# Attention of a two-layer encoder: values with v as the stationary side, divided probabilities, outputs split at once, and a second attention whose head and first output products are interleaved

## The reference

```python
for layer in range(2):
    sh_m, sc_m, g_m, sh_f, sc_f, g_f = split(silu(c) @ ada_w[layer] + ada_b[layer], 6)
    h = rms_norm(x, norm_mix_g[layer]) * (1 + sc_m) + sh_m
    qa, ka, va, qd, kd, vd = split(h @ w_in[layer])          # 2304 columns; rotary on q and k
    ya = window_attention(...)     # 8 query heads of 64, 2 kv heads, +-128 tokens, a sink logit a head
                                   # p = exp(s - m) / (sum(exp(s - m)) + exp(sink - m));  p @ v
    yd = diff_attention(...)       # 4 heads: (softmax_1 - lam * softmax_2) @ v, v of 128 columns,
                                   # then rms_norm over 128 columns, * subln_g * (1 - lambda_init)
    x = x + g_m * (concat(ya, yd) @ w_out[layer])
    h = rms_norm(x, norm_ffn_g[layer]) * (1 + sc_f) + sh_f
    y = swiglu(h)                  # layer 0: dense, 3584 wide
    y = top-2-of-8 expert swiglu   # layer 1: expert weights of 3 x 1024 x 3584 each
    x = x + g_f * y
return rms_norm(x, final_g)
```

## Time and profile before

| what | value |
|---|---|
| time, median of 3 runs | 1364.37 us (1362.79 to 1368.64) |
| the profiled execution, time | 1363.22 us |
| its span in the trace | 1361.5 us |
| TensorE busy | 1288.9 us (95%) |
| VectorE busy | 452.0 us (33%) |
| ScalarE busy | 292.9 us (22%) |
| mean granted clock of TensorE | 0.984 of full speed |
| chain that ended last | PE 82%, DMA 9%, DVE 4%, SPq 2%, ACT 2% |
| traffic | 481.95 MB, mean 354 GB/s |

### The profile page before, as it was taken

One profiled execution on the slowest core, in us unless ns is written; L12 is line 12 of the kernel. 1 busy time (PEld: TensorE's weight loads), 2 busy tenths in 40 slices (PEclk: granted clock), 3 DMA queues, 4 the chain that ended last, 5 costly groups with the idle time before them and its releaser, 6 DMA issues.

```text
span 1361.5 us, 21859 instructions
## 1 busy us (share of the span) xinstructions
PE 1288.9 (95%) x9514; PEld 714.5 (52%) x9515; DVE 452.0 (33%) x808; ACT 292.9 (22%) x524; POOL 32.8 (2%) x82
## 2 busy tenths in 40 slices
PE   5999999999999989996689999999999999899997
PEld 5766888787888677441233333444354333244342
DVE  4876867777459665200100120001001110000011
ACT  3346544443433462110010000010010000010010
POOL 1102100000001010000000000000000000000000
PEclk9999999999999999998789999999999999899999
DMA  9988748888436757999999999999999999999996
GB/s 349 326 338 329 233 176 311 311 297 309 174 123 208 307 204 306 378 408 424 418 421 423 422 421 419 403 408 421 423 419 421 421 424 421 419 420 421 422 423 259
DMA packets 93044, 481.95 MB, mean 354 GB/s; under 512 B 8808, under 2 KB 10928, under 8 KB 63248
## 3 DMA queue, kind: packets, MB, share of 16 engines
q1 hardware_dynamic: 88992, 475.06, 86.9%
q10 hardware_dynamic: 2720, 2.93, 0.8%
q0 software_dynamic: 1232, 2.50, 0.8%
HBM read 477.32 MB, written 1.05 MB: 351 GB/s over the span
## 4 chain that ended last, share of the span: by engine, by line
PE 82%; DMA 9%; DVE 4%; SPq 2%; ACT 2%; issue 1%; POOL 0%; DVEq 0%; ACTq 0%
PE ps L2621 31%; PE ps L2671 15%; PE ps L2304 8%; PE ps L2306 8%; PE ps L2305 8%; DMA raws<-in_moe_w_down_dram 5%; DMA raw<-in_moe_w_gate_dram 2%; DMA weights<-in_ada_w_dram 2%; SPq L891 2%; PE ps L2687 2%; PE ps L2638 1%; DVE weights_lo L1376 1%; PE ps L2594 1%; PE ps L2385 1%; PE ps L2226 1%; PE ps L2370 1%
## 5 line engine op out<-in xcount | busy, mean ns | idle before, releaser
L2621 PE MATMUL ps<-raw,hX 128*32 128x384 f32 (+3 forms) x3840 | 473.0, 543 | 11.8 <-DMA raw<-in_moe_w_up_dram 8.4
L2621 PEld LDWEIGHTS ps<-raw,hX 128*32 128x32 f32 (+1 forms) x3840 | 162.0, 117 | 296.6 <-issue 267.3
L2671 PE MATMUL ps<-raws,m_actT 128*32 128x512 f32 (+1 forms) x1072 | 168.5, 604 | 9.9 <-DMA raws<-in_moe_w_down_dram 9.9
L2304 PE MATMUL ps<-weights_hi,hT_hi 128*128 128x512 f32 (+1 forms) x416 | 162.1, 390 | 2.6 <-DVE hT_lo L1482 1.4
L1797 DVE TENSOR_TENSOR m_act<-m_act,ps 128x512 f32<-128x512 f32 (+1 forms) x28 | 17.4, 621 | 432.0 <-PE ps L2621 431.2
L2306 PE MATMUL ps<-weights_hi,hT_lo 128*128 128x512 f32 (+1 forms) x416 | 159.0, 382 | 0.0
L2305 PE MATMUL ps<-weights_lo,hT_hi 128*128 128x512 f32 (+1 forms) x416 | 158.6, 381 | 0.0
L1376 DVE TENSOR_TENSOR weights_lo<-weights,weights_hi 128x2048 fp32r<-128x2048 f32 (+1 forms) x52 | 113.1, 2202 | 2.3 <-ACT weights_hi L1052 1.1
L2671 PEld LDWEIGHTS ps<-raws,m_actT 128*32 128x32 f32 (+1 forms) x1072 | 52.2, 123 | 116.3 <-issue 103.5
L1052 ACT ACTIVATE weights_hi<-weights 128x2048 fp32r<-128x2048 f32 (+1 forms) x48 | 87.2, 1840 | 55.9 <-PE ps L2306 51.3
L2304 PEld LDWEIGHTS ps<-weights_hi,hT_hi 128*128 128x128 f32 x416 | 78.2, 188 | 21.0 <-issue 4.8
(11 more groups left out here) (282 smaller groups left out, 1084.3 us busy)
## 6 DMA issues: line engine op xcount, KB each, us to landing
raw<-in_moe_w_gate_dram SPq DMA_DIRECT2D x64, 1024.0 KB, 16.5
raw<-in_moe_w_up_dram SPq DMA_DIRECT2D x64, 1024.0 KB, 22.1
raws<-in_moe_w_down_dram SPq DMA_DIRECT2D x32, 2048.0 KB, 24.7
raw<-in_moe_w_gate_dram SPq DMA_DIRECT2D x64, 768.0 KB, 23.3
raw<-in_moe_w_up_dram SPq DMA_DIRECT2D x64, 768.0 KB, 21.1
raws<-in_moe_w_down_dram SPq DMA_DIRECT2D x28, 1536.0 KB, 19.5
weights<-in_ada_w_dram SPq DMA_DIRECT2D x19, 2048.0 KB, 10.0
weights<-in_ffn_w_gate_dram SPq DMA_DIRECT2D x14, 1024.0 KB, 5.1
```

Of the source, the lines that this page charges most:

```text
L2304: pe.matmul(dst, stat_hi, hi, start=start, stop=False, skip_group_check=True)
L2621: mm = pe.matmul(ps[tile * q:tile * q + tile, bank, 0:COL[n]], hX[:, i, at_row:at_row + tile], raw[buffer][:, at:at + COL[n]], start=(i == ...
L2671: mm = pe.matmul(ps[tile * q:tile * q + tile, bank, col:col + w], stationary[:, at_row:at_row + tile], rows_in[:, D * j + w * g:D * j + w ...
```

## The change

1. The two units of a step are no longer taken one after the other. `turn_probs(j, half)` turns four squares; a differential step needs one such turn and one copy (two and two before), a windowed one two and two as before. `PT` has two homes now, `PT_even` over the end of `qk` and `PT_odd`.
2. Windowed steps: VectorE divides the exponentials (`probabilities`, four more operations a step); `values` takes v as stationary side (64 columns, one half of the array a head) and streams 256 columns of turned probabilities, so that the outputs stand in PSUM already turned. ScalarE copies them to `hT_hi` (`window_high`), VectorE writes the difference to `hT_lo` (`head_out`). The turns of half 0 of both tiles with their copies go away. The mask is added to 128 of 256 columns a row.
3. The squares of the differential outputs move from ScalarE to VectorE, at steps 4 and 8; the second tile is normalised at step 9 and turned after the last values. All q/k copies are on ScalarE.
4. `keep` goes. The first output product (0,0) is cut in four and stands among the turns and values of steps 8 and 9. In layer 0 the ADA chunks of steps 6 and 7 move to steps 7 and 8.
5. Layer 1 only (`HEAD_EARLY`): the q/k turns, the scores of steps 0 and 1, their maxima, exponentials and probabilities and one ADA chunk stand among the products (3,1), (4,0), (4,1); its ADA chunks move one step later.
6. The split of the second output chunk's weights: in layer 1 (`OUT_SECOND_EARLY`) the first half stands at step 8 on ScalarE and step 9 on VectorE, the second after the last turned quarter; in layer 0 both halves stand after the last turned quarter.

```diff
-ADA_STEP = [[0, 1, 2, 3, 4, 5, 6, 7], [0, 1, 2, 3]]
+HEAD_EARLY = (False, True)
+ADA_STEP = [[0, 1, 2, 3, 4, 5, 7, 8], [1, 2, 3, 4] if HEAD_EARLY[1] else [0, 1, 2, 3]]
+OUT_SECOND_EARLY = (False, True)
+TURN_PAIRS = [(3, 5, 4, 0, 2, 6, 1) if early else tuple(range(QK_TILES // 2)) for early in HEAD_EARLY]
...
# ScalarE, attention
+                def window_high(k):
+                    act.wait_ge(o_ps, PAIRS * layer + k + 1)
+                    of, to, _ = window_rows(k)
+                    act.activation(to, of, ACT.Copy).then_inc(window_hi, 1)
...
+                for j in range(2 if early else 0, PAIRS + 3):
+                    k = j - 2
                     if j == PAIRS:
-                        turned_high(3 * layer + 1, 0)
                         turned_high(3 * layer + 1, 1)
+                    if 0 <= k < PAIRS:
+                        copy_probs(k, 0)
+                    if k >= 1 and windowed(k - 1):
+                        window_high(k - 1)
+                    if 0 <= k < PAIRS and windowed(k):
+                        copy_probs(k, 1)
                     if j < PAIRS:
+                        exponentials(layer, j)
+                    if j == PAIRS and OUT_SECOND_EARLY[layer]:
+                        straight_part("out", layer, 1, 0)
+                turned_high(3 * layer + 1, 3)
+                if not OUT_SECOND_EARLY[layer]:
+                    straight_part("out", layer, 1, 0)
+                straight_part("out", layer, 1, 1)
...
# VectorE, probabilities and head_out of a windowed step
-                    dve.reciprocal(rec[:, q, :], den[:, q, :]).then_inc(probs_done, 1)
+                    then(dve.reciprocal(rec[:, q, :], den[:, q, :]))
+                    for n in range(4):
+                        i = dve.tensor_scalar(E[:, par, n, :], E[:, par, n, :], rec[:, q, n:n + 1], None, ALU.mult)
+                    i.then_inc(probs_done, 1)
...
+                    dve.wait_ge(window_hi, len(WINDOW_STEPS) * layer + WINDOW_STEPS.index(j) + 1)
+                    of, hi, lo = window_rows(j)
+                    i = dve.tensor_tensor(lo, of, hi.bitcast(F32), ALU.subtract)
...
# VectorE, attention
-                    if j in (5, 9):
+                    if j in (4, 8):
                         t = j // 4 - 1
-                        dve.wait_ge(dsq_done, N_DIFF * (NT * layer + t + 1))
+                        dve.wait_ge(o_done, PAIRS * layer + 4 * t + 2)
...
+                        then(dve.tensor_tensor(square, diff, diff, ALU.mult))
+                        then(dve.reduce_sum(ssq_d[:, four], square.rearrange("p (h n) -> p h n", h=N_DIFF), AX_X))
...
# TensorE, values of a windowed step
+                        for kt in range(NT):
+                            for h in range(2):
+                                mm = pe.matmul(ps[HEAD * h:HEAD * h + HEAD, j % 2, 0:2 * P], v[:, kt, col:col + HEAD],
+                                               turned[:, :, 2 * h + kt, :], start=(kt == 0), stop=(kt == NT - 1),
+                                               skip_group_check=True)
...
# TensorE, the steps
+                    if 0 <= k < PAIRS:
+                        turn_probs(k, 0)
+                    if j == PAIRS:
+                        first_out(range(0, 2))
+                    if k >= 1:
+                        values(k - 1)
                     if j == PAIRS + 1:
-                        pe.wait_ge(mod_ready, 3 * layer + 3)
-                        keep(5, 2)
+                        first_out(range(4, 6))
+                    if 0 <= k < PAIRS and windowed(k):
+                        turn_probs(k, 1)
+                    if j == PAIRS:
+                        first_out(range(2, 4))
+                    if j == PAIRS + 1:
+                        first_out(range(6, KD))
```

More of the change, by code:

```diff
@@ L287, with windowed, turned_at @@
 QK_TILES = 14
+TURN_PAIRS = [(3, 5, 4, 0, 2, 6, 1) if early else tuple(range(QK_TILES // 2)) for early in HEAD_EARLY]
+ROPES_OF_PAIR = (4, 4, 4, 4, 6, 6, 8)
+PAIRS_OF_STEP = ((3, 5), (4, 6), (0, 2), (1, 2))
+BEFORE_HEAD = [IN_ORDER.index((3, 1)) if early else len(IN_ORDER) for early in HEAD_EARLY]
 def pair(i):
     return (i + 4) % 8
+def windowed(j):
+    return pair(2 * j) < 4
+WINDOW_STEPS = [j for j in range(PAIRS) if windowed(j)]
+COPIES_BEFORE = [sum(1 + windowed(i) for i in range(j)) for j in range(PAIRS + 1)]
+def turned_at(n, i):
+    before = 10 * (n // 3) + (0, TURNS, TURNS + NT)[n % 3]
+    return before + (i // 2 if n % 3 == 1 else i) + 1
 Signals = collections.namedtuple(
@@ new lines, in attention_head, with copy_probs @@
+            def attention_head(layer):
+                for i in range(4):
+                    copy_qk(layer, i)
+                if layer == 0:
+                    lambda_exp()
+                straight_part("out", layer, 0, 0)
+                exponentials(layer, 0)
+                copy_qk(layer, 4)
+                copy_qk(layer, 5)
+                straight_part("out", layer, 0, 1)
+                copy_qk(layer, 6)
+                exponentials(layer, 1)
+            def attention(layer):
+                early = HEAD_EARLY[layer]
+                if not early:
+                    for i in range(QK_TILES // 2):
+                        copy_qk(layer, i)
+                def copy_probs(k, half):
+                    act.wait_ge(pt_ps, COPIES_BEFORE[PAIRS] * layer + COPIES_BEFORE[k] + half + 1)
+                    if k >= 2:
+                        act.wait_ge(o_ps, PAIRS * layer + k - 1)
+                    if windowed(k):
+                        to, of = PT[k % 2][:, half], ps[:, 3, :].rearrange("p (k n) -> p k n", k=4)
+                    else:
+                        to, of = PT[k % 2][:, :, 0:2, :], ps[:, 3, :].rearrange("p (e k n) -> p e k n", e=2, k=2)
+                    act.activation(to, of, ACT.Copy).then_inc(pt_done, 1)
+                def window_high(k):
[4 more added lines that the diff above has]
+                    k = j - 2
@@ L1579, in maxima @@
                     h = N_WIN * layer + 2 * m
-                    then(dve.tensor_tensor(rows, rows, mask[:, t, :].unsqueeze(1).broadcast_to([P, 4, SEQ]), ALU.add))
+                    far = slice(P - t * P, 2 * P - t * P)
+                    then(dve.tensor_tensor(rows[:, :, far], rows[:, :, far],
+                                           mask[:, t, far].unsqueeze(1).broadcast_to([P, 4, P]), ALU.add))
                 then(dve.reduce_max(mx[:, q, :], rows, AX_X))
@@ L1624, in attention @@
             def attention(layer):
[L1625 to L1629 removed]
+                for j in range(2 if HEAD_EARLY[layer] else 0, PAIRS + 3):
                     if j < PAIRS:
@@ L1655, in attention @@
                                                      op1=ALU.mult).then_inc(mix_done, 1)
+                    if j == PAIRS + 1 and OUT_SECOND_EARLY[layer]:
+                        low_of("out", layer, 1, 0)
+                    if j == PAIRS + 2:
+                        turned_low(3 * layer + 1, 3)
+                        if not OUT_SECOND_EARLY[layer]:
+                            low_of("out", layer, 1, 0)
                     for c, (of, n) in enumerate(ADA_LATER[layer]):
@@ L2361, in scores_of, with turn_probs @@
                     mm.then_inc(s_ps, 1)
-                def turn_probs(i):
-                    u, j = UNITS * layer + i, i // 2
+                def turn_probs(j, half):
+                    turned = COPIES_BEFORE[PAIRS] * layer + COPIES_BEFORE[j] + half
                     pe.wait_ge(probs_done, PAIRS * layer + j + 1)
-                    if i:
-                        pe.wait_ge(pt_done, u)
-                    for n in range(4 if pair(i) < 4 else 2):
+                    if j or half:
+                        pe.wait_ge(pt_done, turned)
+                    for n in range(4):
+                        row = 2 * (n // 2) + half if windowed(j) else n // 2
@@ L2378, in values @@
                     if j >= 2:
                         pe.wait_ge(o_done, PAIRS * layer + j - 1)
-                    for h in range(2 if m < 4 else 1):
-                        width = HEAD if m < 4 else P
-                        col = (m // 2) * HEAD if m < 4 else P + (m - 4) * P
-                        to = (i % 2) * P + h * width
+                    turned = PT[j % 2]
+                    if windowed(j):
+                        col = (m // 2) * HEAD
                         for kt in range(NT):
-                            mm = pe.matmul(ps[:, j % 2, to:to + width], PT[:, i % 2, 2 * h + kt, :],
-                                           v[:, kt, col:col + width], start=(kt == 0), stop=(kt == NT - 1))
```

227 lines of the change are left out of this document (123 added, 104 removed).

## The result

The changed kernel takes 1368.87 us in the median (20 runs, 1365.04 to 1372.45), the kernel before 1365.39 (20 runs, 1362.79 to 1368.78). The ratio is 1.0021, with a 95% interval from 1.0012 to 1.0031: slower by some 3 us, where 3 us faster was forecast. The profiled execution has a span of 1367.1 us against 1361.5, and a mean granted clock of 0.979 against 0.984.

What follows compares the result with a forecast made beforehand. The start of the experts' weight stream, set by TensorE's chain through both attentions, was taken as the bound. Layer 0 +2.7, layer 1 -7.6 and clock +1.9 give -3.0 us: 1363.8 to 1360.8, range 1355 to 1369.

Steps and rivals of the forecast that it cites:

- the walk: Step-by-step sum of instruction durations through both attentions, to the start of output product (1,0) in each layer.
- 3.67 us for modrow: Layer 0, step 4: TensorE's ADA chunk waits 3.3 us for VectorE's modrow, starting at 109.3 us.
- 4.90 on down_lo: Layer 0, ahead of product (1,0): TensorE idles 4.85 us for the weight split; the product starts at 143.6 us.
- 3.08 ahead of the first output product: Layer 1: TensorE waits some 3 us from 486.5 us for step 6's probabilities.
- layer 1 gains: Layer 1, to the end of product (1,0): 508.35 us against 515.95, a gain of 7.6 us, bounds 5 to 9.
- rival (e): The experts' stream does not follow layer 1, so about half of its 7.6 us is kept: 1364.6 us, chance 0.14.
- (c): VectorE quicker, step 4's modrow no longer delays; layer 0 -0.6, layer 1 -7.6, clock stands: 1355.6 us, chance 0.14.
- (b): The clock stands, so the change gives -4.9 us: 1358.9 us, chance 0.18.
- the clock term: Layer 0, behind the 4.85 us idle: the clock falls and product (1,0) loses 1.9 us, 0 to 4.
- Rival (d): Clock halved at three new waits (two in layer 0, one in layer 1), each costing 4: +7.1, 1370.9 us, chance 0.12.
- the base of all these times: Time of the kernel before, 1363.8 us, taken between the profiled run's 1363.2 and the median of three, 1364.4.
- layer 0 without the clock: Layer 0, start of product (1,0): 143.6 us instead of 140.92, a loss of 2.7 us, 1.5 to 4.8.

Runs made afterwards that it cites:

- no_head: The changed kernel with layer 1's q/k turns and first scores put back behind the last input product, as in layer 0: 1374.14 us, ratio 1.0063.
- fill: The changed kernel with idle 128x128 matmuls (14, 19 and 11) put into three TensorE waits: 1362.13 us, ratio 0.9973.
- again: The changed kernel itself, unaltered, profiled once more: 1364.41 us (one run), no ratio.
- old_pause: The kernel before with three extra unused VectorE reductions ahead of layer 0's modrow at step 4: 1371.97 us, ratio 1.0046.
- mod_first: The changed kernel with layer 0's step 4 modrow computed ahead of step 3's probabilities instead of behind the squares: 1361.48 us, ratio 0.9970.
- out_early: The changed kernel with the first half of layer 0's second output-weight chunk split inside the attention, as in layer 1: 1363.35 us, ratio 0.9987.
- squares_act: The changed kernel with the squares back on ScalarE and the second tile's normalisation at step 10 instead of 9: 1370.12 us, ratio 1.0031.
- fill_half: The changed kernel with about half as many idle matmuls (7, 9 and 5) as fill in the same three waits: 1365.41 us, ratio 0.9999.
- both_heads: fixed plus ScalarE's copy of step 6's turned probabilities ahead of step 7's exponentials, and layer 0's head interleaved, its ADA chunks moved: 1358.64 us, ratio 0.9944.
- swap7: The changed kernel with step 6's probabilities ahead of step 7's maxima on VectorE, both layers: 1367.61 us, ratio 1.0019.
- fixed: The changed kernel with mod_first, out_early and swap7 joined, and the second half of those weights split earlier, both layers: 1354.12 us, ratio 0.9921.

## Why the prediction was wrong

**What held.** The long waits were where and about as long as the walk had put them: 3.67 us for modrow (3.3 forecast), 4.90 on down_lo (4.85), 3.08 ahead of the first output product (3). Windowed values with v as the stationary side take 1.01 us start to start (1.0), the squares 1.53 of VectorE (1.45), the division 1.06 (0.88). Without a fallen clock layer 1 gains 72.27 - 65.06 = 7.2 us (7.6), and no_head and the constant distance to the end show that the experts follow, so rival (e) falls. The modrow wait is there, so (c) falls, and (b) falls with the clock.

**What failed** is the clock term, "I expect the clock to fall there ... 1.9 us lost, 0 to 4", which counted one place. At that place the size was right: from the start of (1,0) to the dense block takes 20.62 us, with filling 18.65, so 1.97. But the clock also fell at step 4 (1.8: from the chunk's start to that of the wait for down_lo 31.8 us, in fill 34.4 of which 4.45 are the filling), behind step 8's wait in layer 1 and behind the wait in the middle of its (1,0) (1.6 each: 15.60 from step 8's turn to the wait for down_lo against 14.02 in fill, 4.62 from that wait's end to the mixing against 3.04; in again, where the clock stood there, 13.99 and 3.04). The four add up to 7.0. Fill's A and B give 6.5, since with the filling the wait for down_lo is 0.2 us longer and step 8's turn stands 0.2 us later; the medians give 6.7. The term held 1.9. With it the error in sign is explained: -4.9 + 1.9 was forecast, and -4.9 + 6.5 would have been +1.6.

The working named the reason against itself. It used a row with 2.8 us idle of 5 that kept the clock as a rule that such waits are safe, though that idle time came in pieces of at most 1.58 us (TensorE's waits at 495.42 and 497.76 us are 1.58 and 1.24), and gave the case of three fallen clocks 0.12 at 4 us each. The row was one draw: old_pause shows the clock low behind the same waits. Rival (d) was the mechanism, with half its price; its +7.1 is too high. Its time, 1370.9, is nearer the 1368.9 than the forecast, in part by luck: the base of all these times, 1363.8, was 1.6 us below the median of 20 runs (1365.39). Of the 8.1 us between forecast and result 1.6 are the base's and 6.5 the change's. That 1368.87 still lies inside the range, by 0.1 us, is owed to the range's width, not to the mechanism.

**The rest** is 0.8 us in layer 1, which without the clock gained 6.8 in fill instead of 7.6, and layer 0 without the clock: fill's 80.40 - 76.24 = 4.2 us lost instead of 2.7. Of the 1.5 more, 0.7 is the start of step 4's chunk (26.66 us behind the first q/k turn; 109.3 - 83.32 = 26.0 forecast), and the tail has two waits of 1.05 and 1.12 us where the walk had one of 1.2.

Together, from fill: 4.2 for layer 0, -6.8 for layer 1 and 6.5 for the clock make +3.9 us; the profiled pair's A and B give +3.9 as well, the medians 3.5.

## What to carry to other kernels

When a step is shortened, list for each engine what stands in its queue ahead of the one small result the bottleneck needs next; here a 0.7 us operation behind some 3 us of division, output and squares cost 5.4 us, and moving one call returned it. Charge a TensorE wait of 2 us or more with a fall of the clock behind it, at every such place and with a chance for the shorter ones, and test it by idle products in the wait before anything is rebuilt. A trade that comes out even may be a gain with a cheap mistake in the order: fix the waits that the change made before judging it.

## What was not expected of the hardware

The same wait does not always have the same effect. Waits of 3.66 to 4.91 us lowered the clock in all eleven cases profiled (in a twelfth it had just fallen); 3.07 or 3.08 us did in four cases of six (mod_first, out_early, no_head and the changed kernel; not in again and squares_act), one of 2.89 and one of 2.77 us did (fill_half, both_heads), waits of 2.10 to 2.16 us did in eight of eleven, while two of 2.45 us (swap7, fixed) did not. Of two waits of 1.99 us in squares_act one did. The Trainium skill, "TensorE: Matmul & The Clock Gate", section "What's actually happening", says that the number of slow products at a kernel's start changes from run to run. Here the same is seen in the middle of a kernel: again had two low stretches fewer, and a span 4.4 us shorter, at waits equal to 0.01 us. It may also be why 6 of the changed kernel's 20 times lie between 1365.0 and 1365.7 and the other 14 between 1367.6 and 1372.5. That the two groups are these cases was not tested, and the spread alone does not show it: the kernel before, with no wait over 1.6 us in its attentions, spreads over 6.0 us.

Idle products of 128 columns, 0.23 us a call, held the clock in fill, where they left 0.5 to 0.7 us of each of three waits, and not in fill_half where they left 2.10 and 2.89 us.
